# Last four down panels of a two-layer block: the column split of the tokens changed from 256 and 256 to 384 and 128

## The reference, cut to what matters

```python
    u = causal_dwconv(h @ w_up, ffn_conv_w)
    gate, up = u[..., :D_FF_2], u[..., D_FF_2:]
    x = x + (jax.nn.silu(gate) * up) @ w_down      # w_down: 2816 x 1024
...
    return rmsnorm(x, final_norm_w)                # x * rsqrt(mean(x*x) + 1e-6) * w, per token
```

## Time and profile before

| | us |
|---|---|
| median of 3 runs | 1444.89 |
| the runs | 1445.23, 1444.89, 1444.48 |
| profiled execution, whole | 1443.01 |
| profiled execution, span | 1440.8 |
| TensorE matmul busy in the span | 1415.7 (98%) |
| VectorE / ScalarE / GpSimd busy | 817.6 / 612.9 / 124.9 |

### The profile page before, as it was taken

The page is one execution under the profiler, slowest core; times in us unless marked ns, Lnnn a source line. Parts: engine busy times, 40 slices in busy tenths (PEclk is TensorE's granted clock), DMA queues, the critical chain, the costliest instruction groups (busy, mean ns, idle before and its releaser), DMA issues.

```text
span 1440.8 us, 20161 instructions
## 1 busy us (share of the span) xinstructions
PE 1415.7 (98%) x7966; PEld 1135.4 (79%) x7966; DVE 817.6 (57%) x1408; ACT 612.9 (43%) x1113; POOL 124.9 (9%) x119
## 2 busy tenths in 40 slices
PE   8999999999999999999999999998999999999998
PEld 6777777788788888888877777776778888888887
DVE  4545555656674343443468767576555663664464
ACT  4544455632362232322335755344444442442234
POOL 0000000012100000000012000440020110110012
PEclk9999999999999999999999999999999999999999
DMA  7222222223223222222223222110332233233222
GB/s 270 76 69 91 88 81 73 70 72 108 88 88 103 98 99 96 91 101 101 89 105 132 89 73 65 54 47 1 103 103 76 100 117 103 88 102 103 84 66 70
DMA packets 41501, 130.94 MB, mean 91 GB/s; under 512 B 4928, under 2 KB 7360, under 8 KB 41408
## 3 DMA queue, kind: packets, MB, share of 16 engines
q1 hardware_dynamic: 40544, 128.60, 26.4%
q10 hardware_dynamic: 864, 1.05, 0.2%
HBM read 124.92 MB, written 4.19 MB: 90 GB/s over the span
## 4 chain that ended last, share of the span: by engine, by line
PE 94%; DVE 3%; ACT 1%; issue 1%; DMA 1%; POOL 0%; SPq 0%; POOLq 0%; DVEq 0%; ACTq 0%
PE bank L1303 91%; PE bank L1306 3%; DVE Fm L2058 1%; ACT Fm L1700 1%; DVE Fm L2066 0%; DVE Fm L2163 0%; DMA Fm<-in_x_dram 0%; DMA Fm<-in_relb_dram 0%; POOL Fm L2662 0%; SPq L2759 0%; ACT Whi L1700 0%; POOL Xf L2662 0%; ACT Rm L1700 0%; DVE Fm L2063 0%; DVE Rm L2066 0%
## 5 line engine op out<-in xcount | busy, mean ns | idle before, releaser
L1303 PE MATMUL bank<-Rm,Whi 128*128 128x512 f32 (+1 forms) x2840 | 873.9, 389 | 9.4 <-ACT Whi L1700 6.1
L1303 PEld LDWEIGHTS bank<-Rm,Whi 128*128 128x128 f32 x2840 | 532.5, 188 | 120.5 <-ACT Whi L1700 6.1
L1303 PE MATMUL bank<-Rm,Wlo 128*128 128x512 f32 (+1 forms) x1420 | 565.0, 398 | 1.7 <-issue 1.5
L2058 DVE TENSOR_TENSOR Wlo<-Wraw,Whi 128x1024 fp32r<-128x1024 f32 (+2 forms) x225 | 284.0, 1266 | 111.7 <-ACT Whi L1700 111.0
L1303 PEld LDWEIGHTS bank<-Rm,Wlo 128*128 128x128 f32 x1420 | 267.4, 188 | 61.6 <-issue 7.9
L1700 ACT ACTIVATE Whi<-Wraw 128x1024 fp32r<-128x1024 f32 (+2 forms) x225 | 232.5, 1038 | 186.7 <-PE bank L1303 181.4
L1303 PE MATMUL bank<-Xr,Whi 128*128 128x512 f32 (+1 forms) x760 | 228.4, 382 | 0.0
L2662 POOL TENSOR_TENSOR Fm<-Fm 128x512 f32<-128x512 f32 (+1 forms) x89 | 102.4, 1158 | 778.8 <-ACT Fm L1700 487.6
L1700 ACT ACTIVATE Fm<-bank 128x512 f32<-128x512 f32 (+4 forms) x200 | 92.5, 483 | 166.2 <-PE bank L1303 102.2
L1303 PEld LDWEIGHTS bank<-Xr,Whi 128*128 128x128 f32 x760 | 141.1, 188 | 27.8
L1303 PE MATMUL bank<-Xr,Wlo 128*128 128x512 f32 (+1 forms) x380 | 145.5, 383 | 0.0
(11 more groups left out here) (100 smaller groups left out, 717.0 us busy)
## 6 DMA issues: line engine op xcount, KB each, us to landing
Wraw<-in_w_in_dram SPq DMA_DIRECT2D x67, 512.0 KB, 3.3
Wraw<-in_w_ff_dram SPq DMA_DIRECT2D x64, 512.0 KB, 3.2
Wraw<-in_w_up_dram SPq DMA_DIRECT2D x44, 512.0 KB, 3.2
Wraw<-in_w_o_dram SPq DMA_DIRECT2D x16, 512.0 KB, 3.3
Wraw<-in_w_down_dram SPq DMA_DIRECT2D x16, 512.0 KB, 3.2
Wraw<-in_w_ab_dram SPq DMA_DIRECT2D x8, 512.0 KB, 3.2
Wraw<-in_w_down_end_dram SPq DMA_DIRECT2D x8, 384.0 KB, 3.1
Fm<-in_relb_dram SPq DMA_DIRECT2D x8, 256.0 KB, 5.7
```

The lines of the kernel that those rows point to most:

```text
L1303: return e.matmul(o, l, r, start=first, stop=last)
L2058: return e.tensor_tensor(o, x, y, op)
```

## The change

`EARLIER` grows from two to three of the four blocks of 128 tokens, `LATER` shrinks from two to one. All that is written in terms of these two slices follows: the widths of the matmuls, adds, squares, scalings and stores. `rms_tiles` and `rms_cols` say which blocks a statistic covers, and the start and stop flags of the statistic's matmuls follow them. The number of panel matmuls, of scalings and of stores stays the same.

```diff
-        EARLIER, LATER = slice(0, 256), slice(256, 512)
+        EARLIER, LATER = slice(0, 384), slice(384, 512)
...
         def rms_tiles(t_):
-            return tiles4()[:2] if t_ == 4 else tiles4()[2:] if t_ == 5 else tiles4()
+            return tiles4()[:3] if t_ == 4 else tiles4()[3:] if t_ == 5 else tiles4()
...
         def rms_cols(t_):
-            return (0, 2) if t_ == 4 else (2, 4) if t_ == 5 else (0, 4)
+            return (0, 3) if t_ == 4 else (3, 4) if t_ == 5 else (0, 4)
...
-                        x = mm(b[:, t:t + 1], F(SUM2)[:, s], mean_m[:, 0:1], t_ < 4 or t % 2 == 0, t_ < 4)
+                        x = mm(b[:, t:t + 1], F(SUM2)[:, s], mean_m[:, 0:1], t_ < 4 or t in (0, 3), t_ < 4)
...
-                            x = mm(b[:, t:t + 1], F(SQ + sq_rank(t_, 7) % 3)[:, s], mean_m[:, 0:1], False, t % 2 == 1)
+                            x = mm(b[:, t:t + 1], F(SQ + sq_rank(t_, 7) % 3)[:, s], mean_m[:, 0:1], False, t > 1)
```

## The result

| us | before | after |
|---|---|---|
| median of 6 runs each | 1444.68 (1442.78 to 1447.29) | 1455.17 (1452.41 to 1457.27) |
| ratio, 95% interval | | 1.0065 (1.0054 to 1.0076) |
| profiled execution, whole | 1443.01 | 1456.17 |
| its span | 1440.8 | 1453.9 |
| its mean granted TensorE clock | 1.000 | 0.990 |

What follows compares the result with a forecast made beforehand. TensorE's matmuls, busy 98% of the span at full clock, were taken as the bound, with link latency and stores in the tail. 3.84 - 0.27 + 0.67 - 2.0 = +2.2 us on 1444.89 gave 1447.1, range 1444.8 to 1449.0.

Steps and rivals of the forecast that it cites:

- `EARLIER`, +3.84: Last four EARLIER panels on TensorE: 72 matmuls widened from 256 to 384 columns, +3.84 us.
- `LATER`, -0.27: LATER panels on TensorE: 72 matmuls at 128 columns, limited by weight loads, 0.116 us each, -0.27 us (-0.54 to 0).
- Statistic and rows, +0.67: TensorE's queue between LATER panels: extra instructions in rmsstat 4 (+0.45) and rmsrows 4 (+0.22), +0.67 us.
- VectorE, 0 to 0.05: EARLIER scalings, now 384 wide: VectorE just keeps up with the panels' adds, 0 to +0.05 us.
- Tail, -2.0: From last add to span end: shorter links (-0.81) and half the store bytes (-1.20), -2.0 us (-2.35 to -0.8).
- The stores: LATER stores in the tail: 512 B packets at 29.5 ns each, 1.89 us instead of 3.09, -1.20 us.
- The third rival: LATER stores cost by packet, not byte, staying at 3.09 us; sum +3.4, 1448.3 us; chance 0.15.
- The first rival: LATER weight loads hide behind short streams, matmuls giving back their columns, VectorE then limiting; +0.3, 1445.2 us; chance 0.12.
- The second rival: LATER's short reduced-format matmuls cost up to the 512-column pace, 0.227 us; sum +10.2, 1455.1 us; chance 0.11.
- a pace over 0.126: Profile sign of a wrong forecast: LATER matmuls over 0.126 us each, where 0.112 to 0.120 was expected.

Runs made afterwards that it cites:

- e2: Kernel before with the EARLIER matmuls of the last four panels streaming 384 columns, the added ones computed again in LATER; 1448.96 against 1444.84 us, ratio 1.0026.
- e9: Kernel after with rmsstat 4, rmsrows 4 and EARLIER's scalings and stores behind all LATER panels, and every LATER matmul issued twice; 1463.6 us.
- e1: Kernel after with LATER matmuls streaming 256 columns, of which only the last 128 are used; 1447.46 against 1444.84 us for the kernel before, ratio 1.0019.
- e7: Kernel after without the unused matmul ahead of rmsrows 5; 1452.24 us.
- e12: Kernel after with LATER panels 4 and 5 streaming 256 columns, 6 and 7 128; 1448.42 against 1445.38 us for the kernel before, ratio 1.0021.
- e4: Kernel after with rmsstat 4 moved behind panel 6, rmsrows 4 and all eight EARLIER scalings and stores behind panel 7; 1450.38 us.
- e8: Kernel after with rmsstat 4, rmsrows 4 and all eight EARLIER scalings and stores behind the last LATER panel; 1451.15 us.
- e6: Mirror of the change's split: 128 columns in EARLIER and 384 in LATER, statistics, scalings and stores following; 1448.33 us.
- e3: Kernel before with LATER matmuls streaming only tokens 384 to 511, products of 256 to 383 left out; 1450.77 against 1444.84 us, ratio 1.0033.
- e10: Kernel after with two unused 512-column float32 matmuls right behind rmsstat 4; 1449.07 against 1445.55 us for the kernel before, ratio 1.0028.

## Why the prediction was wrong

- **`EARLIER`, +3.84:** right. +3.88 in the trace of the kernel after, and +3.8 by e2 alone (2.5 to 5.2 by its interval).
- **`LATER`, -0.27:** this step failed. It bounded the pace of a 128-column matmul between 0.1125 and 0.120 us and multiplied by 72, which takes the full granted clock for granted; the earlier trace rows show that clock for a kernel whose `LATER` streams 256 columns. At full clock the pace is 0.111 to 0.112 us, just under the lower bound, and the weight load is the limit as argued: the twelve single-column instructions, which have hardly anything to stream, take as long (1.31 / 12 = 0.109). The term came to -0.6 + 5.1 = +4.5. The Trainium skill's page "TensorE: Matmul & The Clock Gate", section "LDWEIGHTS (loading the stationary operand)", has a load take its columns divided by 1.2 in ns, 107 for these 128; e9's 144 matmuls took 111 ns each.
- **What stood in its place:** from panel 5 on the clock was 0.50. That is +5.1 on 50 matmuls and +0.6 on `rmsrows 4`. With the -0.6 of the pace, and the statistic and rows at +0.6 before the clock, the stretch came to +5.70 where the prediction's terms for it make +0.40.
- **Statistic and rows, +0.67:** right in their counts. The twelve instructions take 1432.25 to 1433.56 = 1.31 us; the rows cost more by the clock alone.
- **VectorE, 0 to 0.05:** right, seen in e1, where its scalings end 0.01 us before the last add starts; at half clock it has room.
- **Tail, -2.0:** right at full clock (-1.9 in e1), -0.55 in the kernel after. Of the 1.45 that are missing 0.9 is the unused matmul, which at half clock is no longer covered by the statistic's small steps (e7).
- **The stores:** 512 B packets go at 265 GB/s at a share of 0.94, 16 x 512 B x 0.94 / 265 GB/s = 29.1 ns for a packet against the 29.5 of the prediction. The third rival falls.
- **The first rival** falls too: nothing runs at 0.067 us.
- **The second rival** named 1455.1 us and 1455.2 came, but by another mechanism: it held a short matmul to be dear in itself, and had the rows and the tail at their full pace. That the numbers agree is luck. Its pace of 0.227 was seen (0.213), at half clock only. Of the prediction's signs of being wrong, "a pace over 0.126" was the one that showed.

No execution shows the change itself at full clock; the terms measured at full clock give 3.88 - 0.6 + 0.6 - 1.9 = +2.0, an estimate, and e12's undisturbed execution, with half of its `LATER` matmuls wide, shows +2.2. The fall of the clock makes the rest of the 9.0, some 7 us. The 9.0 of the traces agrees with the 9.4 of the ratio.

**The cause.** Shown: narrow matmuls alone hold the clock (e4, e8, e9, e6, one execution each); the statistic among 256- or 384-column matmuls holds it (before, e1, e6, e12); the statistic with narrow matmuls on both sides is followed by the fall (after, e3, e4, e7), and so is that of e10, where the narrow ones stand ahead of it. Up to panel 7, e4 and e8 differ only in the place of the statistic: with it the clock falls there, without it 72 narrow matmuls hold it. TensorE waited for nothing ahead of the fall in panel 5. The same page of the Trainium skill, section "HAM oscillation — how this bites in real kernels", tells of a clock that falls where TensorE waits between bursts for data; no run here shows such a wait ahead of that fall, so the measurement decides that waits aren't needed for one. Open: what the chip weighs in a narrow matmul beside a single-column one. Whether the single column or the float32 format of the statistic is what counts was not tried apart; e10 gives a hint against the format, since its `rmsrows 4`, six float32 instructions of 128 columns, stands between narrow panels at 1.00. The place of the fall is open too: it came 1.1 us (e4) to 2.2 us (e3, 1424.17 to about 1426.35) after the statistic's first matmul, in e9 4.2 us after it. And e10 shows that T4 in its form "wide matmuls next to the statistic hold the clock" is too strong, since behind it they only brought the clock back.

## What to carry to other kernels

A matmul with fewer columns saves next to nothing once its weight load is the limit: here 128 columns take 0.111 us where 256 take 0.120. Before narrowing a stretch, look at which single-column matmuls (here the statistic) stand in it, and keep them among wide ones, as e1 and e12 do. Price a changed stretch at both levels of the clock, and what follows it too: the 2.2 us predicted here became 9.0. When a result is off by more than the sum of the bounds, read the granted clock by stage before any engine's durations.

## What was unexpected of the hardware

- The granted clock can fall while TensorE's matmuls are busy without a break (3.75 of 3.75 us), and multiplying more can be faster: e1 streams 256 columns where the change streams 128, and takes 2.7 us over the kernel before instead of 9.4.
- The clock also falls in some executions far from the change, where TensorE has small gaps. The profiled ones show two places: 1000 to 1020 us (kernel after, e8, e9, e12, a clock of 0.74 to 0.91 over it; in the kernel after it cost 4 us) and 740 to 760 us (e1, e2, e7, e9, 0.91 over it, with TensorE busy for 19.7 of the 20 us). Both places lie far ahead of what any of the edits touches. In the three groups of rounds the kernel before has six executions with a mean clock of 1.000, 1442.92 to 1443.31 us, and those with 0.995 or 0.996 took 1446.1 to 1448.5: most of its spread goes with this clock. Where it fell in them was not profiled.
